# A decoder step on one core: projecting keys, queries, values in this order, and loading attention's first tiles during the last block

## The chip, the cores and the metric

One core of a Trainium2 chip runs the whole program. The metric is the device time of one execution in microseconds (us). Engine names: PE or TensorE (matmuls), PEld (its weight loads), DVE or VectorE, ACT or ScalarE, POOL or GpSimd, SP or SyncE (here it only issues transfers, "DMAs"). Each engine works through its own list of instructions in order and waits for the others by semaphores.

## The reference: what is computed

One inference step of a two-layer decoder for a prompt of 1024 tokens and eight sample tokens (1032 columns, width 1024). Layer 0 is a pooling mixer and a ConvFFN. Then one shared set of keys and values is projected, and layer 1 uses it with queries of its own in a dilated sliding-window attention with three groups of eight heads, followed by a second ConvFFN. What matters for the change:

```python
kv = einsum('btd,de->bte', rms_norm(x, g_kv), w_kv)       # keys and values, 3 groups x 8 heads x 64
k = rotary(rms_norm(kv[:, :, 0], k_gain), pos)            # keys: norm per head, then rotation
v = kv[:, :, 1]                                           # values: neither
q = einsum('btd,de->bte', rms_norm(x, g), w_q)
q = rotary(rms_norm(q, q_gain), pos) * (HEAD_DIM ** -0.5) # queries: like keys
```

The attention scores a block of 128 queries against its own block of keys and, in groups 0 and 1, the one before it, adds a mask, takes the exponential and weighs the values.

## The kernel before, in words

**Projection** (`pe_project`, `act_project`, `dve_project`, `pool_project`, `sp_project`; lines 1126 to 1372). Three groups `g`; in each three blocks `u`: keys (0), values (1), queries (2); in each nine tiles `t`: eight of 128 tokens and one with the eight sample rows. A full tile is 48 matmuls (two halves of 256 columns, eight slices of the width, three products of high and low parts; lines 1356 to 1358), the sample tile 32 narrower ones (lines 1352, 1353). The order of the last tiles is (7, half 0), (8, half 0), (7, half 1), (8, half 1). A tile's result lies in PSUM bank `t % 3`; a bank is free for tile `t + 3` when VectorE has written the row to `kn[t % 3]` (semaphore `pj_v`).

A key or query tile then goes a long way: ScalarE squares (L1240), VectorE sums per head (L1289), ScalarE takes a square root (L1243), VectorE refines it (L459 to L465, L1294) and scales into `kn` (L1297), GpSimd multiplies by the gain and rotates (L1321 to L1329), and SyncE stores the tile in device memory, in `kvs` or `qs` (L1157). A value tile needs one VectorE operation (L1283) and the store. A sample tile has ahead of that a ScalarE copy (L1224) and a VectorE sum (L1266). In each block ScalarE and VectorE also split four pieces of weights for the next block, at tiles 3, 5 and 7 (`pj_piece`, L1204 and L1206); SyncE loads them behind the stores of tiles 2, 5 and 8 (L1142). In the last group the last block splits and loads none. On TensorE group 0 is written out and groups 1 and 2 are a loop; on SyncE, ScalarE and VectorE groups 0 and 1 are the loop and the last group is written out.

**Attention** (`sp_attention`, `pe_attention`, `dve_attention`, `act_attention`, `pool_attention`). 24 steps `s` of one tile of queries and one of keys and values, 48 half steps `i` of four heads. TensorE transposes queries (`turn_q`) and keys (`turn_k`) into bank 7 (L1521), VectorE copies them to `qT` and `kT` (L1645), TensorE puts the mask (L1544) and the scores (L1552) into banks 0, 1 or 2, 3; VectorE takes the maxima (L1653), ScalarE the exponentials (L1760), TensorE transposes the probabilities (L1563) and multiplies by the values (L1579). Beside this GpSimd and VectorE multiply and sum the sample rows (L1782, L1681), from copies that SyncE loads.

SyncE's list behind the last projection store: it waits for TensorE's last projection matmul, for all weight pieces, and for all stores to have landed (L1433). Then it issues `load_q(0)` (L1439), `load_kv(0)` (L1445), `load_q(1)`, the masks (L1461), seven small loads of sample rows (L1463 to L1465), and in the loop over steps `load_q(s + 1)`, `load_kv(s)`, the store of step `s - 3` (L1510) and the sample rows' loads (L1452, L1455). From the third on, `load_q(s)` waits until the transposes of the queries two steps back are done; from the fifth on, `load_kv(s)` waits for outputs. VectorE begins the attention with four conversions, of the unit matrix and of the masks to bf16 (L1633 to L1639), for which it waits until the masks have landed; only then does it copy the first transposed queries. Masks, unit matrix and the tiles lie in SBUF over `xh` and `xl`, the projection's input, so they can't be filled before its last matmul.

Of the kernel before, what the change touches and what calls it, by code (L numbers as in the profile page):

```python
# [17 lines left out]
P = 128  # L18
# [6 lines left out]
KC = D // P  # L25
# [10 lines left out]
GROUPS = 3  # L36
# [21 lines left out]
def build(nc, a, o):  # L58

    with ExitStack() as ctx:  # L60
# [50 lines left out]
        osb = sb("osb", [P, 3, OW], F32, r1)  # L111
        maskf = sb("maskf", [P, 3, P], F32, r1)
        mask = sb("mask", [P, 3, QW], BF16, r1)
        identb = sb("identb", [P, P], BF16, r1)
        qn = sb("qn", [NS, GROUPS, QW], F32, r1)
# [51 lines left out]
        r2.close()  # L167
        wph, wpl = (wp0h, wp1h, wp2h), (wp0l, wp1l, wp2l)

        r2 = ExitStack()  # L170
# [955 lines left out]
        def pj_src(u, half, part, g, later):  # L1126
            cols = slice(half * HW, (half + 1) * HW)
            if u == 2:
                w = a["w_q"][0].rearrange("(k p) (g n) -> g p k n", p=P, g=GROUPS)
            else:  # L1130
                w = a["w_kv"].rearrange("(k p) (c g n) -> c g p k n", p=P, c=2, g=GROUPS)[u]
            return w[later:][bass.ds(g, 1), :, 4 * part:4 * part + 4, cols].rearrange("o p k n -> p (o k) n")

        def sp_project(sp):
# [9 lines left out]
            def body(g, last):  # L1144
                for u in range(3):
                    for t in range(9):
                        G = 27 * g + 9 * u + t
                        M = MT[t]
                        if u == 0 and t == 5:
                            sp.wait_ge(pj_l, 12 * g + 6)  # L1150
                        if u == 1:
                            sp.wait_ge(pj_v, G + (K0 + 1))
                        else:
                            sp.wait_ge(pj_r, 5 * (18 * g + (9 if u else 0) + t + 1))
                        rows = slice(t * P, t * P + M)
                        dst = qs[bass.ds(g, 1), rows, :] if u == 2 else kvs[bass.ds(g, 1), rows, u, :]
                        sp.dma_start(dst.rearrange("o p n -> (o p) n"), kn[0:M, t % 3, :]).then_inc(rows_out[t % 3], 16)  # L1157
                        for m in {2: [4 * u + 7], 5: [4 * u + 8], 8: [4 * u + 9, 4 * u + 10]}.get(t, []):
                            if m < 12 or not last:
                                load(m, g, free=(m == 8))  # L1160
# [24 lines left out]
        def pj_piece(e, g, m, act):  # L1185


            u, H, part = m % 12 // 4, m // 2, m % 2
            gain = G_ATTN if u == 2 else G_KV
            if act:  # L1190
# [25 lines left out]
        def act_project(act):  # L1216
# [9 lines left out]
            def body(g, last):  # L1226
                for u in range(3):
                    for t in range(9):
                        for m in pieces_at(u, t, last):
                            pj_piece(act, g, m, True)  # L1230
                        M, G = MT[t], 27 * g + 9 * u + t
                        if u != 1:
                            Q = 18 * g + (9 if u else 0) + t
                            act.wait_ge(pj_pe, G + 1)
                            act.wait_ge(pj_v, K0)
                            act.wait_ge(pj_s, 7 * Q + 1)
                            if t == 8:
                                sample_low(g, u)
                                act.wait_ge(pj_k, 6 * g + 2 * u + 2)
                            nc.scalar.activation(sq[0:M, 0, 0:QW], srow if t == 8 else ps[0:M, t % 3, :], ACT.Square,  # L1240
                                                 scale=rtok[0:M, t:t + 1]).then_inc(pj_sq, 1)
                            act.wait_ge(pj_s, 7 * Q + 3)
                            nc.scalar.activation(hs[0:M, 2, :], hs[0:M, 1, :], ACT.Sqrt).then_inc(pj_rt, 1)  # L1243
                        elif t == 8:
                            act.wait_ge(pj_pe, G + 1)
                            sample_low(g, u)
# [5 lines left out]
        def dve_project(v):  # L1252
# [16 lines left out]
            def body(g, last):  # L1269
                for u in range(3):  # L1270
                    for t in range(9):
                        for m in pieces_at(u, t, last):
                            pj_piece(v, g, m, False)
                        M, G = MT[t], 27 * g + 9 * u + t
                        b = t % 3
# [4 lines left out]
                        row = srow if t == 8 else ps[0:M, b, :]  # L1280
                        if u == 1:
                            v.wait_ge(pj_pe, G + 1)
# [20 lines left out]
            body(GROUPS - 1, True)  # L1303

        def pool_project(q):
            for i in range(3):
                q.wait_ge(rows_out[i], 16)
            half = HEADS * 8
            with q.Fori(0, GROUPS) as g:
                for u in (0, 2):  # L1310
                    for t in range(9):
# [101 lines left out]
        def wides(i):  # L1413
# [11 lines left out]
                    for r in range(T - WIN[g], N, P)]  # L1425

        def sp_attention(sp):

            sp.wait_ge(pj_pe, 27 * GROUPS)
            sp.wait_ge(pj_h, 12 * GROUPS)  # L1430
            sp.wait_ge(pj_l, 12 * GROUPS)
            for i in range(3):
                sp.wait_ge(rows_out[i], ROWS)  # L1433

# [22 lines left out]

            load_q(0)
            load_kv(0)
            load_q(1)  # L1460
            sp.dma_start(maskf[:, :, :], a["masks"]).then_inc(in_mask, 16)  # L1461
            for g in range(GROUPS):
# [3 lines left out]
            for s in range(NSTEP + 3):  # L1466
                if 1 <= s < NSTEP:
                    if s + 1 < NSTEP:
                        load_q(s + 1)
                    load_kv(s)  # L1470
                if s >= 3:
# [46 lines left out]
        def pe_attention(pe):  # L1518
# [5 lines left out]
            def turn_q(s):  # L1524
                pe.wait_ge(at_q[s % 2], moved(s, 2))
                wait(pe, at_tc, 2 * s)
                turn(qt[:, s % 2, :], s)

            def turn_k(s):
                pe.wait_ge(at_kv[s % 4], moved(s, 4))  # L1530
                pe.wait_ge(at_tc, 2 * s + 1)
                turn(kvt[:, s % 4, 0:QW], s)

            def scores(i):
# [5 lines left out]
                if i == 0:  # L1540
                    pe.wait_ge(at_mk, 4)
                m = 0 if wide(i) else (2 if STEPS[s][0] == 2 else 1)
                for c in range(2):
# [23 lines left out]
            def outputs(i):  # L1567
# [5 lines left out]
                for j in range(4):  # L1573
                    h = 4 * (i % 2) + j
                    tiles = [(s - 1) % 4, s % 4] if wide(i) else [s % 4]
                    for w, slot in enumerate(tiles):
                        n = j * len(tiles) + w
                        v = kvt[:, slot, QW + h // 2 * P:QW + (h // 2 + 1) * P]
                        mm = pe.matmul(ps[:, 6, j * P:(j + 1) * P], probT[:, i % 2, n * P:(n + 1) * P], v,  # L1579
# [51 lines left out]
        def dve_attention(v):  # L1631
            v.wait_ge(in_mask, 16)
            nc.vector.tensor_copy(identb[:, :], ident[:, :]).then_inc(at_mk, 1)  # L1633
            for m in range(3):
                if m == 0:
                    ins = nc.vector.tensor_copy(mask[:, 0, :].rearrange("p (w n) -> p w n", w=2),
                                                maskf[:, 0:2, :].rearrange("p c n -> p (c n)").unsqueeze(1).to_broadcast([P, 2, 2 * P]))
                else:
                    ins = nc.vector.tensor_copy(mask[:, m, 0:2 * P].rearrange("p (w n) -> p w n", w=2),  # L1639
                                                maskf[:, m, :].unsqueeze(1).to_broadcast([P, 2, P]))  # L1640
                ins.then_inc(at_mk, 1)

            def turned(s, k):
# [480 lines left out]
```

## Time and profile before

| | |
|---|---|
| time, median of 3 | 2437.13 us (2436.57 to 2438.08) |
| profiled execution | 2431.53 us, its span 2429.7 us |
| mean granted TensorE clock | 0.981 |
| TensorE busy | 2328.6 us, 96% of the span |
| VectorE, ScalarE, GpSimd busy | 1287.9, 758.5, 261.8 us |
| transfers | 273.34 MB, mean 112 GB/s |
| chain of work that ended last | PE 70%, issue 13%, POOL 6%, DVE 5%, DMA 3% |

Times of rows are in microseconds from the start of the span, durations of groups in nanoseconds where they say so. The busy time of a stretch tells which engine could bound it; the timeline tells when an instruction started, how long it took, and in brackets how long its engine had been idle before it and what ended that. "L1297" is a line of the kernel printed above; numbers such as "x2" count the instructions that are merged in a row, and the duration is then that of all of them.

### The profile page before, as it was taken

What the parts mean: (1) busy time and instruction counts of PE and PEld (TensorE: products, weight loads), DVE (VectorE), ACT (ScalarE), POOL (GpSimd) and SP (SyncE); (2) the same over time, 40 slices, a digit from 0 to 9 for tenths busy, and PEclk for the clock granted to TensorE, in tenths of its full rate; (3) what the DMA queues carried; (4) which work ended last, traced back from release to release, by engine and by line L of the source; (5) the groups of instructions that cost most, each with busy time, mean ns of one, the idle gap of its engine ahead of it and who ended that gap; (6) DMA issues with size and microseconds to landing.
All of it is one profiled execution on the core that took longest, in us unless ns stands there. A gap on an engine that the chain in (4) does not pass through costs nothing.

```text
span 2429.7 us, 41646 instructions
## 1 busy us (share of the span) xinstructions
PE 2328.6 (96%) x16141; PEld 2270.4 (93%) x16141; DVE 1287.9 (53%) x2088; ACT 758.5 (31%) x1345; POOL 261.8 (11%) x346
## 2 busy tenths in 40 slices
PE   7999999999999999999996989788999999999999
PEld 7899999999999899999996876587999999999999
DVE  5754554555455563645534775545545545554445
ACT  5422222223344431313212543232222222243333
POOL 1200000000011041523413220120000000000000
PEclk8999999999999999999998999899999999999999
DMA  5112212214654612222223787411222222245555
GB/s 172 35 52 78 78 52 78 78 53 144 199 169 153 210 54 97 84 97 71 79 71 112 240 254 205 162 33 44 59 71 78 61 69 78 59 148 190 192 169 175
DMA packets 198861, 273.34 MB, mean 112 GB/s; under 512 B 12424, under 2 KB 143800, under 8 KB 198483
## 3 DMA queue, kind: packets, MB, share of 16 engines
q1 hardware_dynamic: 193954, 267.09, 35.0%
q10 hardware_dynamic: 4792, 4.68, 0.6%
q8 instruction: 78, 1.28, 0.2%
q14 instruction: 37, 0.30, 0.0%
HBM read 218.19 MB, written 61.26 MB: 115 GB/s over the span
## 4 chain that ended last, share of the span: by engine, by line
PE 70%; issue 13%; POOL 6%; DVE 5%; DMA 3%; ACT 1%; SPq 1%; POOLq 0%; DVEq 0%; ACTq 0%
PE ps L337 43%; PE ps L814 18%; POOL kn L1321 3%; PE ps L1579 2%; PE ps L1552 1%; POOL sq L1323 1%; DMA kvt<-kvs 1%; POOL kn L1329 1%; PE ps L1563 1%; PE ps L1521 1%; PE ps L1591 1%; PE ps L646 1%; POOL sq L1324 1%; POOL sq L1326 1%; DVE rb L945 1%
## 5 line engine op out<-in xcount | busy, mean ns | idle before, releaser
L337 PE MATMUL ps<-xh,whl 128*128 128x344 f32 x4320 | 805.8, 321 | 16.2 <-DVE whl L777 11.9
L337 PEld LDWEIGHTS ps<-xh,whl 128*128 128x128 f32 x4320 | 703.2, 188 | 18.5 <-DVE whl L777 12.7
L337 PE MATMUL ps<-xl,whl 128*128 128x344 f32 x2160 | 459.3, 321 | 0.0
L814 PE MATMUL ps<-gdh,whl 128*128 128x384 f32 (+1 forms) x1568 | 377.7, 322 | 6.6 <-ACT ctm L898 3.0
L337 PEld LDWEIGHTS ps<-xl,whl 128*128 128x128 f32 x2160 | 366.6, 189 | 0.0
L814 PEld LDWEIGHTS ps<-gdh,whl 128*128 128x128 f32 x1568 | 273.6, 188 | 8.7 <-DVE gdl L983 3.8
L772 ACT ACTIVATE whl<-stage 128x1024 fp32r<-128x1024 f32 x88 | 93.1, 1060 | 515.0 <-DMA stage<-in_w_up 280.4
L814 PE MATMUL ps<-gdl,whl 128*128 128x384 f32 (+1 forms) x784 | 250.9, 320 | 0.0
L907 DVE TENSOR_TENSOR ub<-ps,rb 128x1032 f32<-128x1032 f32 x44 | 54.2, 1232 | 236.8 <-PE ps L337 236.8
L777 DVE TENSOR_TENSOR whl<-stage,whl 128x1024 fp32r<-128x1024 f32 x88 | 107.3, 1221 | 122.8 <-ACT whl L772 122.8
L814 PEld LDWEIGHTS ps<-gdl,whl 128*128 128x128 f32 x784 | 147.4, 188 | 0.0
L980 DVE TENSOR_TENSOR whl<-stage,whl 128x1024 fp32r<-128x1024 f32 x66 | 80.8, 1224 | 117.6 <-ACT whl L989 117.4
L814 PE MATMUL ps<-gdh,wx 128*128 128x384 f32 (+1 forms) x544 | 134.5, 316 | 0.0
L1760 ACT ACTIVATE prob<-ps,osb 128x128 f32<-128x128 f32 (+1 forms) x192 | 77.2, 414 | 140.1 <-DVE osb L1653 140.1
L1356 PE MATMUL ps<-wp0h,xh 128*128 128x256 f32 x384 | 110.1, 287 | 8.2 <-DVE x L999 6.0
L989 ACT ACTIVATE whl<-stage 128x1024 fp32r<-128x1024 f32 x66 | 70.0, 1060 | 136.4 <-PE ps L814 113.5
L922 DVE SCALAR_TENSOR_TENSOR cb<-ub,cwT,cb 128x1024 f32<-128x1024 f32 x88 | 112.4, 1277 | 0.0
L922 DVE SCALAR_TENSOR_TENSOR ca<-ua,cwT,ca 128x1024 f32<-128x1024 f32 x88 | 112.3, 1276 | 0.0
L1358 PE MATMUL ps<-wp0h,xl 128*128 128x256 f32 x384 | 110.1, 287 | 0.0
L1357 PE MATMUL ps<-wp0l,xh 128*128 128x256 f32 x384 | 109.4, 285 | 0.0
L907 DVE TENSOR_TENSOR ua<-ps,rb 128x1032 f32<-128x1032 f32 x44 | 54.2, 1233 | 101.9 <-PE ps L337 101.8
L1358 PE MATMUL ps<-wp1h,xl 128*128 128x256 f32 x384 | 108.2, 282 | 0.0
(258 smaller groups left out, 3970.3 us busy)
## 6 DMA issues: line engine op xcount, KB each, us to landing
stage<-in_w_down SPq DMA_DIRECT2D x100, 512.0 KB, 3.6
stage<-in_w_up SPq DMA_DIRECT2D x88, 512.0 KB, 5.3
gs<-cb SPq DMA_DIRECT2D x44, 516.0 KB, 3.1
graw<-gs SPq DMA_DIRECT2D x88, 192.0 KB, 3.6
rb<-in_w_down SPq DMA_DIRECT2D x32, 512.0 KB, 3.5
stage<-in_w_kv SPq DMA_DIRECT2D x24, 512.0 KB, 4.1
kvs<-kn SPq DMA_DIRECT2D x48, 256.0 KB, 2.0
kvt<-kvs SPq DMA_DIRECT2D x16, 512.0 KB, 4.6
```

Source lines behind the costliest of these rows:

```text
L337: mm = pe.matmul(ps[:, bank0 + c, 0:NW], w, m[:, c * NW:(c + 1) * NW], start=(i == 0), stop=(i == len(parts) - 1))
L772: nc.scalar.activation(wh[:, half, :], stage[:, half, :], ACT.Copy).then_inc(f_hi, 1)
L777: nc.vector.tensor_tensor(wl[:, half, :], stage[:, half, :], wh[:, half, :].bitcast(F32), ALU.subtract).then_inc(f_lo, 1)
L814: mm = pe.matmul(ps[:, d, 0:n], wt_, m, start=(f == 0 and i == 0), stop=(f == NF - 1 and i == 2))
L907: nc.vector.tensor_tensor(cols3(u[:, 2:2 + N]), bank3(half), cols3(rb[:, :]), ALU.mult).then_inc(S.B if half else S.A, 1)
L922: nc.vector.scalar_tensor_tensor(out=c[:, 0:T], in0=u[:, t:t + T], scalar=w, in1=c[:, 0:T], op0=ALU.mult, op1=ALU.add).then_inc(S.conv, 1)
L980: nc.vector.tensor_tensor(wdl[slot], draw[slot], wdh[slot].bitcast(F32), ALU.subtract).then_inc(f_dl, 1)
L1321: nc.gpsimd.tensor_tensor(row, row, per_head(hg[0:M, 1 if u else 0, :], HD), ALU.mult).then_inc(pj_r, 1)
L1356: pe.matmul(out, xh[:, k, tok], W[:, k, :], start=(k == 0), stop=False)
L1357: pe.matmul(out, xh[:, k, tok], Wt[:, k, :], start=False, stop=False)
L1358: mm = pe.matmul(out, xl[:, k, tok], W[:, k, :], start=False, stop=(k == KC - 1))
L1760: ins = nc.scalar.activation(prob[:, i % 2, j * n:(j + 1) * n], src[:, j % 2, j // 2, :], ACT.Exp, bias=osb[:, s % 3, QW + h:QW + h + 1], ...
```

## The change

The order of the blocks becomes keys, queries, values: `u` is 1 for queries and 2 for values in all five engines' projection functions. The masks, the unit matrix in bf16, the first queries (`qt0`) and the first keys and values (`kvt0`, over `rb`) get places that are free during the last block, and their loads stand in SyncE's list behind the store of the last block's tile 3, the four conversions in VectorE's list ahead of its tile 6. SyncE's attention list then starts with `load_q(1)` and `load_kv(1)`, for which it waits only for TensorE's last projection matmul, and waits for weight pieces and stores after these. TensorE's first two half steps wait for the last projection tiles to have left the banks. The diff, without the lines that only rename:

```diff
-        maskf = sb("maskf", [P, 3, P], F32, r1)
-        mask = sb("mask", [P, 3, QW], BF16, r1)
-        identb = sb("identb", [P, P], BF16, r1)
...
+        r2 = ExitStack()
+        sb("over_wp1", [P, 2 * KC, HW], F32, r2)
+        mask = sb("mask", [P, 3, QW], BF16, r2)
+        identb = sb("identb", [P, P], BF16, r2)
+        maskf = sb("maskf", [P, 3, P], F32, r2)
+        qt0 = sb("qt0", [P, QW], F32, r2)
+        r2.close()
+        kvt0 = rb[:, 0:2 * QW]
...
-            if u == 2:
+            if u == 1:
                 w = a["w_q"][0].rearrange("(k p) (g n) -> g p k n", p=P, g=GROUPS)
             else:
-                w = a["w_kv"].rearrange("(k p) (c g n) -> c g p k n", p=P, c=2, g=GROUPS)[u]
+                w = a["w_kv"].rearrange("(k p) (c g n) -> c g p k n", p=P, c=2, g=GROUPS)[u // 2]
...
                         sp.dma_start(dst.rearrange("o p n -> (o p) n"), kn[0:M, t % 3, :]).then_inc(rows_out[t % 3], 16)
+                        if last and u == 2 and t == 3:
+                            sp_first_tiles(sp)
...
-                        if u != 1:
+                        if u != 2:
                             Q = 18 * g + (9 if u else 0) + t
                             act.wait_ge(pj_pe, G + 1)
...
+                        if last and u == 2 and t == 6:
+                            dve_masks(v)
                         M, G = MT[t], 27 * g + 9 * u + t
...
+        def dve_masks(v):
+            v.wait_ge(in_mask, 16)
+            nc.vector.tensor_copy(identb[:, :], ident[:, :]).then_inc(at_mk, 1)
+            for m in range(3):
...
-                for u in (0, 2):
+                for u in (0, 1):
...
+        def q_tile(s):
+            return qt[:, s % 2, :] if s else qt0
+
+        def kv_tile(s):
+            return kvt[:, s % 4, :] if s else kvt0
+
+        def sp_first_tiles(sp):
+
+            for i in range(3):
+                sp.wait_ge(rows_out[i], 16 + 16 * 9)
+            sp.dma_start(maskf[:, :, :], a["masks"]).then_inc(in_mask, 16)
+            sp.dma_start(qt0[:, :], qs[0, 0:P, :]).then_inc(at_q[0], 16)
+            sp.dma_start(kvt0, kvs[0, 0:P].rearrange("t c n -> t (c n)")).then_inc(at_kv[0], 16)
+
         def sp_attention(sp):
 
             sp.wait_ge(pj_pe, 27 * GROUPS)
-            sp.wait_ge(pj_h, 12 * GROUPS)
-            sp.wait_ge(pj_l, 12 * GROUPS)
-            for i in range(3):
-                sp.wait_ge(rows_out[i], ROWS)
...
-            load_q(0)
-            load_kv(0)
             load_q(1)
-            sp.dma_start(maskf[:, :, :], a["masks"]).then_inc(in_mask, 16)
+            load_kv(1)
+            sp.wait_ge(pj_h, 12 * GROUPS)
+            sp.wait_ge(pj_l, 12 * GROUPS)
+            for i in range(3):
+                sp.wait_ge(rows_out[i], ROWS)
...
-                    load_kv(s)
+                    if s > 1:
+                        load_kv(s)
...
                 if i == 0:
                     pe.wait_ge(at_mk, 4)
+                if i < 2:
+                    pe.wait_ge(pj_v, 27 * GROUPS + K0 - 1 + i)
...
         def dve_attention(v):
-            v.wait_ge(in_mask, 16)
-            nc.vector.tensor_copy(identb[:, :], ident[:, :]).then_inc(at_mk, 1)
-            for m in range(3):
```

The waits of `sp_first_tiles` are for the stores of group 0, two groups back. The line `pj_v, 27 * GROUPS + K0 - 1 + i` stands for value tile 7 at the first half step and for the sample rows' values at the second.

## Rows read from the trace of the kernel before

**Rows 1.** Busy us (instructions) of PE, PEld, DVE, ACT, POOL; clock, DMA share, GB/s.

```profile
900.00:1000.00 100.00, 100.00 (x848) 99.83 (x847) 46.85 (x120) 23.23 (x54) 26.15 (x45) 1.00 0.26 88
1200.00:1299.20 99.20, 99.17 (x839) 98.75 (x837) 38.38 (x105) 16.08 (x38) 24.87 (x45) 1.00 0.18 60
1301.70:1325.20 23.50, 7.33 (x36) 5.23 (x37) 7.38 (x18) 3.84 (x12) 5.64 (x11) 0.50 0.40 118
```

**Rows 2.** Timeline of TensorE over the seam: start, us, engine, line, operation, tiles.

```profile
1298.90 0.28 PE L1353 MATMUL ps<-wp2l,xs 128*40 128x256 f32 x1
1313.54 1.12 PE L1521 MATMUL ps<-ident,qt 128*128 128x128 f32 x4 [14.36 <-DMA qt<-qs]
1318.21 1.08 PE L1521 MATMUL ps<-ident,kvt 128*128 128x128 f32 x4 [3.56 <-DVE qT L1645]
1320.08 0.61 PE L1544 MATMUL ps<-mask,identb 128*128 128x256 bf16 x2 [0.78 <-DVE kT L1645]
1321.77 1.11 PE L1521 MATMUL ps<-ident,qt 128*128 128x128 f32 x4
1324.40 1.10 PE L1521 MATMUL ps<-ident,kvt 128*128 128x128 f32 x4
1327.92 0.65 PE L1521 MATMUL ps<-ident,qt 128*128 128x128 f32 x4
```

**Rows 3.** Timeline of the other engines and of SyncE's issues over the seam.

```profile
1300.43 0.69 DVE L1297 TENSOR_TENSOR kn<-ps,hs 128x512 f32<-128x512 f32 x1
1310.81 0.35 SPq L1439 DMA_DIRECT2D qt<-qs  x1
1316.50 0.23 DVE L1633 CAST identb<-ident 128x128 bf16<-128x128 f32 x1 [10.17 <-DMA maskf<-in_masks]
1317.38 0.68 DVE L1645 COPY qT<-ps 128x512 f32<-128x512 f32 x1
```

**Rows 4.** The chain that ended last, over the seam: start, us, what.

```profile
1309.27 1.46 DMA qs<-kn
1312.15 4.33 DMA maskf<-in_masks
```

**Rows 5.** Timeline around the jump in TensorE's loop, and group 1's sample queries.

```profile
1149.82 0.38 PE L1356 MATMUL ps<-wp0h,xh 128*128 128x256 f32 x1 [2.18 <-issue]
1155.32 0.68 DVE L1297 TENSOR_TENSOR kn<-sq,hs 8x512 f32<-8x512 f32 x1
```

**Rows 6.** Timeline of a value block; L1240's first and last start; weight pieces.

```profile
919.45 1.67 DVE L1206 SCALAR_TENSOR_TENSOR wp1l<-stage,gT,wp1h 128x256 fp32r<-128x256 f32 x4
1240.70 0.75 DVE L1283 TENSOR_SCALAR kn<-ps,rtok 128x512 f32<-128x512 f32 x1 [4.94 <-PE ps L1358]
1251.14 0.59 ACT L1224 ACTIVATE sq<-ps 8x512 f32<-8x512 f32 x1 [2.46 <-DVE kn L1283]
1252.54 0.47 DVE L1283 TENSOR_SCALAR kn<-sq,rtok 8x512 f32<-8x512 f32 x1
L1240 ACT ACTIVATE sq<-ps,rtok x48: 667/688/690, 859.4 to 1297.4; 128x512 f32<-128x512 f32 x48
```

**Rows 7.** Landing of query tiles (L1439) and of key/value tiles (L1445).

```profile
DMA to landing us min/median/max: 2.7/5.1/9.2
...
DMA to landing us min/median/max: 3.6/4.9/9.9
```

**Rows 8.** Two gaps of TensorE in the attention, and the clock behind the first.

```profile
1406.04 0.66 PE L1521 MATMUL ps<-ident,kvt 128*128 128x128 f32 x4 [2.23 <-DMA kvt<-kvs]
1407.40:1410.65 3.25, 3.25 (x20) 2.78 (x18) 1.80 (x5) 0.95 (x3) 1.27 (x1) 0.50 0.34 122
1453.26 0.60 PE L1544 MATMUL ps<-mask,identb 128*128 128x512 bf16 x2 [2.77 <-DVE kT L1645]
```

**Rows 9.** Waits in the attention: who, for whom, us in all, times, longest.

```profile
SPq L1510 <- DVE osb L1664: 65.3, 14, 9.6
PE ps L1521 <- DMA kvt<-kvs: 9.4, 4, 5.6
```

More of the change, by code:

```diff
@@ L1150, in body @@
                             sp.wait_ge(pj_l, 12 * g + 6)
-                        if u == 1:
+                        if u == 2:
                             sp.wait_ge(pj_v, G + (K0 + 1))
@@ L1155, in body @@
                         rows = slice(t * P, t * P + M)
-                        dst = qs[bass.ds(g, 1), rows, :] if u == 2 else kvs[bass.ds(g, 1), rows, u, :]
+                        dst = qs[bass.ds(g, 1), rows, :] if u == 1 else kvs[bass.ds(g, 1), rows, u // 2, :]
                         sp.dma_start(dst.rearrange("o p n -> (o p) n"), kn[0:M, t % 3, :]).then_inc(rows_out[t % 3], 16)
+                        if last and u == 2 and t == 3:
+                            sp_first_tiles(sp)
                         for m in {2: [4 * u + 7], 5: [4 * u + 8], 8: [4 * u + 9, 4 * u + 10]}.get(t, []):
@@ L1188, in pj_piece @@
             u, H, part = m % 12 // 4, m // 2, m % 2
-            gain = G_ATTN if u == 2 else G_KV
+            gain = G_ATTN if u == 1 else G_KV
             if act:
@@ L1280, in body @@
                         row = srow if t == 8 else ps[0:M, b, :]
-                        if u == 1:
+                        if u == 2:
                             v.wait_ge(pj_pe, G + 1)
@@ L1303, in dve_project @@
             body(GROUPS - 1, True)
+        def dve_masks(v):
+            v.wait_ge(in_mask, 16)
+            nc.vector.tensor_copy(identb[:, :], ident[:, :]).then_inc(at_mk, 1)
+            for m in range(3):
+                if m == 0:
+                    ins = nc.vector.tensor_copy(mask[:, 0, :].rearrange("p (w n) -> p w n", w=2),
+                                                maskf[:, 0:2, :].rearrange("p c n -> p (c n)").unsqueeze(1).to_broadcast([P, 2, 2 * P]))
+                else:
+                    ins = nc.vector.tensor_copy(mask[:, m, 0:2 * P].rearrange("p (w n) -> p w n", w=2),
+                                                maskf[:, m, :].unsqueeze(1).to_broadcast([P, 2, P]))
+                ins.then_inc(at_mk, 1)
         def pool_project(q):
@@ L1526, in turn_q @@
                 wait(pe, at_tc, 2 * s)
-                turn(qt[:, s % 2, :], s)
+                turn(q_tile(s), s)
             def turn_k(s):
@@ L1531, in turn_k @@
                 pe.wait_ge(at_tc, 2 * s + 1)
-                turn(kvt[:, s % 4, 0:QW], s)
+                turn(kv_tile(s)[:, 0:QW], s)
             def scores(i):
@@ L1574, in outputs @@
                     h = 4 * (i % 2) + j
-                    tiles = [(s - 1) % 4, s % 4] if wide(i) else [s % 4]
-                    for w, slot in enumerate(tiles):
+                    tiles = [s - 1, s] if wide(i) else [s]
+                    for w, tile in enumerate(tiles):
                         n = j * len(tiles) + w
-                        v = kvt[:, slot, QW + h // 2 * P:QW + (h // 2 + 1) * P]
+                        v = kv_tile(tile)[:, QW + h // 2 * P:QW + (h // 2 + 1) * P]
                         mm = pe.matmul(ps[:, 6, j * P:(j + 1) * P], probT[:, i % 2, n * P:(n + 1) * P], v,
@@ L1631, in dve_attention @@
         def dve_attention(v):
-            v.wait_ge(in_mask, 16)
-            nc.vector.tensor_copy(identb[:, :], ident[:, :]).then_inc(at_mk, 1)
-            for m in range(3):
[L1635 to L1641, printed above, removed]
             def turned(s, k):
```

## The prediction

> **What bounds the kernel now.** I began with the busy time by stretch [rows 1]. Up to 1299.20 us TensorE is busy all the time (99.17 of 99.20 us) at the full clock; behind it, from 1301.70 to 1325.20, it is busy for 7.33 of 23.50 us. The projection is bound by TensorE, the seam behind it is not. Next I read TensorE's own timeline over the seam [rows 2]: the last projection matmul ends at 1298.90 + 0.28 = 1299.18, the first query transposes start at 1313.54, the key transposes at 1318.21, and the first scores (with their mask) at 1320.08. So 1320.08 - 1299.18 = 20.90 us pass between the projection's end and the first scores.
>
> What fills them is in the chain of waits and in the timelines of the other engines [rows 3, 4]. Queries are projected last, so the normalization and rotation of their last two tiles lie at the end: tile 7's queries leave VectorE at 1300.43 + 0.69 = 1301.12, the eight sample rows go the same way one after another through ScalarE, VectorE and GpSimd, and their store starts at 1309.27 and lands at 1309.27 + 1.46 = 1310.73. Only then does SyncE issue the first loads: queries at 1310.81, then keys/values, and masks at 1312.15. The first tile is there at 1313.5, the masks at 1312.15 + 4.33 = 1316.48, and VectorE, which must convert the masks before it copies anything for TensorE, copies the first queries at 1317.38.
>
> **The change part by part.**
>
> *Order keys, queries, values.* The same matmuls, the same operations for each tile; TensorE's projection keeps its length if it meets no new wait. New is that a query block follows a key block inside a loop body: two blocks with the long chain side by side. The trace already has this neighbourhood between groups (queries, then the next group's keys). There the sample rows' keys or queries are finished at 1155.32 + 0.68 = 1156.00 [rows 5]; the block had ended at 1147.64 (1149.82 less the idle 2.18), that is 8.4 us earlier. TensorE wants that bank (three banks, nine tiles) at the next block's tile 2, two tiles or 11.4 us behind the block's end (48 matmuls of a tile at 848 in 100 us [rows 1] are 5.66 us). So 3.0 us are to spare, without counting the 2.18 us of the loop's jump. Cost 0; the cover is TensorE's own work on two tiles.
>
> *What is left behind the last matmul.* Now the last block is values: tile 7 needs one VectorE operation, which starts about when the corresponding ScalarE one did, 1297.4 [rows 6], and takes 0.75. The sample rows take ScalarE copy, VectorE sum, VectorE scale: from 1251.14 to 1252.54 + 0.47 = 1253.01, 1.87 us [rows 6]. TensorE's results are visible some 0.2 us after 1299.18, so VectorE is free at 1299.4 + 1.87 = 1301.3. GpSimd and the square root drop out of the path.
>
> *First tiles, masks.* The three loads are issued after value tile 3, some four and a half tiles (25 us) ahead of the end, against a slowest landing of 9.9 us for such tiles and 4.33 for the masks [rows 4, 7]. In the projection's last part SyncE only stores. Their three issues (0.35 us for one, [rows 3]) stand ahead of the store of value tile 4, which comes a tile later (5.66 us): nobody waits. The four conversions (1317.38 - 1316.50 = 0.88 us, [rows 3]) move ahead of value tile 6, where VectorE is idle for 4.94 us in each tile [rows 6]. All this costs 0.
>
> *The new seam, summed.* TensorE transposes the first queries right at 1299.2 (0.65 us at the full clock, 1.12 at the lower). VectorE copies them at 1301.3 (0.68) to 1302.0; TensorE takes 0.15 to start (1318.21 - 1317.38 - 0.68, [rows 2, 3]): keys' transposes at 1302.15. From there to the first scores it is as before, 1320.08 - 1318.21 = 1.87: 1304.0. The value tiles 7 and 8, whose banks the first scores now wait for, are done by 1298.2 and 1301.3. Gain 1320.08 - 1304.0 = **16.1 us**.
>
> *The clock.* It was at the lower level, 0.50 (1.2 of 2.4 GHz), from 1301.70 to 1325.20 [rows 1], after 2.5 us of idleness and until 5.1 us into steady work. The new seam holds two idle pieces of some 2.3 and 1 us. The trace has both outcomes for such a gap: after 2.23 us idle the clock was 0.50 for 3.25 us, after 2.77 us it stayed at 1.00 [rows 8]. At 1.00 the keys' transposes and copy would be 0.45 shorter (0.65 for 1.12, [rows 2]). The first two half steps take TensorE 1324.40 - 1321.77 = 2.63 us each now, and half of that at 1.00; but VectorE's reduce, copy, reduce, copy of some 0.68 each [rows 3] behind about 1.1 us of scores then ends last, at 3.9 us (an estimate from these rows), against 5.3: 1.4 us, or up to 2.0 with the later transposes. So the clock adds 0 (as low as before) to 0.45 + 2.0 = 2.5 us. I take 0.5: the first 5 us behind 1301.7 look much as before, with short work between waits. The Trainium skill (TensorE: Matmul & The Clock Gate, The HAM clock gate) states that the throttled level is the default and that sustained activity releases it; by that alone the start would run low, and the sum would stay at 16.1. The gap of 2.77 us that left the clock high shows that a gap of this size does not settle it.
>
> *Who is next.* SyncE stores the sample values at 1301.35 (0.3), then tile 1's queries at about 1301.8 and its keys/values at 1302.2, landing at best 2.7 and 3.6 us later [rows 7]: 1304.5 and 1305.8. They are wanted at 1304.0 + (1321.77 - 1320.08) = 1305.7 and 1304.0 + (1324.40 - 1320.08) = 1308.3 [rows 2]. Then SyncE waits for the sample store (1301.4 + 1.5 = 1302.9, over by then) and issues the seven small loads, at 0.35 each [rows 3] 2.4 us, and tile 2's queries at about 1305.0, landing at 1307.7 to 1310.1 (median 5.1); wanted at 1304.0 + (1327.92 - 1320.08) = 1311.9. Everything later hangs on TensorE's progress: SyncE waited 65.3 us for the outputs of steps whose rows it stores [rows 9], so the loads move along with them, as does the sample rows' work. The stage's later waits for transfers (9.4 us, [rows 9]) move and are not filled. The layer behind it starts from the attention's end.
>
> *Exit from TensorE's loop.* Before, whatever it cost lay under 14.36 us of waiting. Bounds: the jump back cost 2.18 us [rows 5], running into the loop, between 998 and 1000, nothing (TensorE is busy for all of the 100 us to 1000, [rows 1]); leaving is nearer to the latter, as no jump is taken, so 0. If 2.18: transposes end at 1302.5 instead of 1299.9, VectorE copies 1.2 us later than summed. The Trainium skill (Runtime: NRT & Kernel Launch, Instruction fetch mechanics) says that a taken branch can force a fetch of the target, and that running on is prefetched; by that rule it is 0.
>
> *Sum.* 16.1 + 0.5 = **16.6 us**. The profiled execution took 2431.53 (span 2429.7), the timed ones 2437.13; I carry the difference in us over: 2437.13 - 16.6 = **2420.5**, and 2413.1 for the new span. A change within 0.2% (4.9 us) is about what a measurement can't tell from none.
>
> **The rivals.**
>
> *Clock high throughout the new start:* 16.1 + 2.5 = 18.6 us, 2418.5. For it: the 2.77 us gap. Against: the low clock at the old seam began 2.5 us after the end of steady work. Chance 0.10.
>
> *SyncE late with tile 2 or tile 1.* All small loads now stand between the value tile and tile 2's queries, close to their use. If those take the slowest landing, 9.2 us [rows 7], they arrive at 1314.2 instead of 1311.9, 2.3 us late; tile 1's keys/values at 9.9 would be 3.8 late. Some 4 us gone: gain 12.6, 2424.5. For it: landing times grow where tiles share the queues; against: these come before the sample loads start. Chance 0.09.
>
> *Given back in the transfer-bound part.* Later in the stage TensorE waits four times for keys and values, 5.6 us at most [rows 9]. If transfers there don't keep pace with the earlier start and one more such wait appears, the gain is 16.6 - 5.6 = 11, 2426. Against: all issues follow TensorE's events. Chance 0.05.
>
> *No change, since something else holds the start,* for instance a wait at the first scores for a late projection tile in place of the old ones. It would have to last over 11.7 us; the value chain's length of 1.87 speaks against. 2436. Chance 0.02.
>
> *Slower.* The long chain in two neighbouring blocks falls behind TensorE. A tile's chain now runs from ScalarE's 1297.4 to 1300.43 + 0.69 = 1301.12, 3.7 us, plus weight pieces (four of 1.67 us in nine tiles, [rows 6]), 4.5 in all against 5.66 per tile. Above 5.66 a backlog grows; over 8 tiles in each of 3 groups it eats the 16.6 us from 5.66 + 16.6/24 = 6.35 us on. If GpSimd, ScalarE and VectorE, now active together for two blocks on end, slowed each other to 6.5 per tile: 24 x 0.84 = 20.2 lost, 3.6 us slower, 2440.7. Against: query blocks next to key blocks keep up today. Chance 0.02.
>
> **How the numbers follow.** The forecast has 0.72: 2420.5, its own range 2418.5 to 2423 (loop exit 1.2, landing times 1, clock 2). With the high clock (0.10) below and SyncE's lateness (0.09) above, 2417.5 to 2425.0 leaves out the giving back, no change, slower and some of each end, under 2 in 10. Faster by over 0.2%: 0.72 + 0.10 + 0.09 + 0.05 less a little of the last, 0.95; within 0.2%: 0.03; slower: 0.02.
>
> **What would show it.** Right: TensorE busy throughout the projection with its end unmoved near 1299; first query transposes within 0.3 us; first scores 4.8 us behind the end; no wait for the masks; the rest of the attention shifted as a block. Wrong: idle time of the projection's matmuls behind VectorE in the query block; TensorE waiting for tile 1 or tile 2; more than 9.4 us of waiting for keys/values later; the interval from first scores to the attention's end longer than before.

## The result, and the profile after

| | before | after |
|---|---|---|
| median | 2437.61 us (2436.57 to 2440.27, 4 runs) | 2416.97 us (2411.69 to 2420.93, 4 runs) |
| ratio | | 0.9917 (95%: 0.99 to 0.9933) |
| profiled execution, its span | 2431.53, 2429.7 us | 2411.69, 2409.9 us |
| mean granted clock | 0.981 | 0.985 |

The forecast was 2420.5 in 2417.5 to 2425.0. The change is faster, as forecast, but 20.6 us in place of 16.6, and 0.5 us below the range. Two later comparisons gave ratios of 0.9922 (0.9908 to 0.9937) and 0.993 (0.9913 to 0.9947), gains of 17.1 and 17.4 us by medians. So part of the 20.6 is scatter: over all comparisons single executions of the kernel before lie up to 15 us apart (2428.99 to 2443.86), those of the changed kernel up to 12 (2411.63 to 2423.23). The three comparisons together give some 18.4 us, 1.8 above the forecast. The rest of this text is about where the traces differ from the forecast's terms.

TensorE's timeline over the new seam, to be read against [rows 2] (columns as there; `rb` is now the first keys and values):

```profile
1297.91 0.28 PE L1374 MATMUL ps<-wp2l,xs 128*40 128x256 f32 x1
1298.03 0.60 PE L1555 MATMUL ps<-ident,qt 128*128 128x128 f32 x4
1300.85 0.63 PE L1555 MATMUL ps<-ident,rb 128*128 128x128 f32 x4 [2.22 <-DVE qT L1670]
1302.27 0.39 PE L1580 MATMUL ps<-mask,identb 128*128 128x256 bf16 x2 [0.79 <-DVE kT L1670]
1303.73 1.11 PE L1555 MATMUL ps<-ident,qt 128*128 128x128 f32 x4
1306.24 0.66 PE L1555 MATMUL ps<-ident,kvt 128*128 128x128 f32 x4
1307.93 0.38 PE L1580 MATMUL ps<-mask,identb 128*128 128x512 bf16 x1 [0.59 <-DVE kT L1670]
```

The 14.36 us of waiting are gone, the query transposes follow the last matmul at once, and the first scores start at 1302.27, 4.08 us behind 1297.91 + 0.28 = 1298.19. The other engines and SyncE, to be read against [rows 3, 4]:

```profile
1298.23 0.59 ACT L1231 ACTIVATE sq<-ps 8x512 f32<-8x512 f32 x1 [42.44 <-PE ps L1374]
1298.92 0.68 DVE L1273 TENSOR_TENSOR sq<-sq,ps 8x512 f32<-8x512 f32 x1 [1.71 <-ACT sq L1231]
1299.63 0.47 DVE L1292 TENSOR_SCALAR kn<-sq,rtok 8x512 f32<-8x512 f32 x1
1300.03 0.67 DVE L1670 COPY qT<-ps 128x512 f32<-128x512 f32 x1
1300.47 0.35 SPq L1470 DMA_DIRECT2D qt<-qs  x1
1300.86 0.43 SPq L1476 DMA_DIRECT2D kvt<-kvs  x1
```

The chain is the one of the forecast: ScalarE copy, VectorE sum, VectorE scale, then the copy of the first queries; no masks, no GpSimd. The busy time by stretch, against [rows 1], with the clock in the third column from the right:

```profile
1200.00:1298.20 98.20, 98.20 (x833) 98.06 (x832) 45.52 (x119) 16.83 (x39) 32.42 (x56) 1.00 0.20 71
1298.20:1302.20 4.00, 1.06 (x8) 0.61 (x6) 2.43 (x4) 1.87 (x2) 0.00 (x0) 1.00 0.29 89
1302.20:1306.30 4.10, 4.04 (x25) 3.01 (x26) 1.39 (x3) 1.51 (x8) 0.00 (x0) 0.58 0.87 243
```

In this trace the clock stays high through the seam's waits and falls to 1.2 GHz behind them, in the first two half steps. And the waits of the later attention, against [rows 9]:

```profile
SPq L1544 <- DVE osb L1689: 63.0, 14, 9.1
PE ps L1555 <- DMA kvt<-kvs: 8.2, 5, 4.4
```

8.2 us of waiting for keys and values where 9.4 had been: nothing was given back there.

To see where the whole difference lies, I cut each trace at the same instructions: first and last matmul of the projection, first scores, first scores of the third half step, last scores, first output projection matmul, end. Lengths in us, for three traces of either kernel (two later ones of each from the experiments):

| stretch | before, 3 traces | after, 3 traces | mean difference |
|---|---|---|---|
| ahead of the projection | 846.8, 850.4, 850.2 | 847.8, 850.8, 852.0 | +1.1 |
| projection | 452.4, 452.5, 452.4 | 450.4, 448.8, 450.3 | -2.6 |
| seam | 20.90, 21.67, 21.45 | 4.08, 4.07, 4.07 | -17.3 |
| two half steps | 6.21, 5.59, 5.78 | 5.67, 6.45, 5.39 | 0.0 |
| rest of the attention | 211.2, 214.0, 210.8 | 209.6, 213.0, 214.5 | +0.3 |
| merge of the groups | 60.3, 62.3, 60.0 | 60.6, 61.9, 61.6 | +0.5 |
| output projection, second ConvFFN | 832.0, 831.8, 831.9 | 831.8, 832.5, 831.8 | +0.2 |

Only two rows differ by more than they scatter: seam and projection. The sum is -17.8 us, in agreement with the later comparisons.

### The profile page after: what moved, and what is told of

It is laid out like the page before. It is cut to its first block, busy times and chain, and to the rows that moved or that the text cites. A ratio compares the mean times of both kernels' runs of the same rounds, so it can differ in the third digit from the quotient of the medians.

```text
span 2409.9 us, 41632 instructions
## 1 busy us (share of the span) xinstructions
PE 2326.3 (97%) x16130; PEld 2269.7 (94%) x16141; DVE 1294.0 (54%) x2088; ACT 759.3 (32%) x1345; POOL 263.3 (11%) x346
## 4 chain that ended last, share of the span: by engine, by line
PE 89%; DVE 5%; DMA 3%; ACT 1%; SPq 1%; issue 1%; POOL 0%; DVEq 0%; ACTq 0%; POOLq 0%
PE ps L342 44%; PE ps L819 18%; PE ps L1379 6%; PE ps L1377 6%; PE ps L1378 6%; PE ps L1615 2%; PE ps L1588 1%; DMA kvt<-kvs 1%; PE ps L1627 1%; PE ps L1599 1%; PE ps L1555 1%; PE ps L651 1%; PE ps L1374 1%; PE ps L1373 1%; DVE rb L950 1%
```

## The experiments

Theory A: the seam alone makes the gain, the rest is a clock term taken too small and scatter. Theory B: the new order itself shortens the projection. Later, J: what the order gives in the projection lies in one place, the jump of TensorE's loop; against it K: the jump's part is chance, and the order works elsewhere.

**The two kernels again.** Unchanged.

> The kernel before once more, against itself. Theory A (the changed seam alone makes the gain; the 4 us above the forecast are a clock term taken too small and scatter between executions): ratio 1.000, and its timed runs scatter by some 4 us; in the trace the seam from the last projection matmul to the first scores is again 20.9 us within 0.3, while the stretches outside of it differ from the first trace by up to 2 us in sum. Theory B (the new order itself shortens the projection by 2 us): the projection's length, first to last matmul, is 452.4 us again within 0.3.

> The changed kernel once more, five rounds. A: ratio 0.9925 to 0.993 (a gain of 17 to 18.5 us: seam 16.8, clock in the first half steps 0 to 2), not the 20.6 of the first medians; the seam 4.1 us; the projection's length 451 to 453. B: the projection's length 450.4 again within 0.3, the gain 19.5 to 21 us, ratio 0.9915 to 0.992.

Measured: the kernel before against itself 1.0007 (0.9994 to 1.002), its ten runs from 2428.99 to 2443.86 us; the kernel after 0.9922. The projections were 452.5 and 448.8 us. The seam of before was 21.67, 0.8 longer, which A had not allowed; that of after 4.07. The scatter is larger than I had thought, and B had the better of it on the projection, though its number, 450.4 again, was missed too, and the ratio is A's. The projection must be looked at block by block.

**Order alone.** The diff of `pj_src`, `sp_project`, `pj_piece`, `act_project`, `dve_project` and `pool_project`, nothing of the loads:

```diff
-                        if u != 1:
+                        if u != 2:
                             Q = 18 * g + (9 if u else 0) + t
...
-                for u in (0, 2):
+                for u in (0, 1):
```

> Only the order keys, queries, values; first loads and masks as before. Both theories take the seam as the sum of a chain: the sample values leave VectorE 2.1 us behind the last matmul, their store lands 1.8 us later, and from there 9.35 us pass to the first scores as before (1320.08 - 1310.73): 13.2 us in place of 20.9. A: gain 7.7 us, ratio 0.9968. B: 9.7 us, ratio 0.9960, the projection 2 us shorter.

Measured: ratio 0.9961 (0.9946 to 0.9975), seam 13.88 us for 13.2 expected, projection 448.8. TensorE over its seam:

```profile
1307.56 1.11 PE L1521 MATMUL ps<-ident,qt 128*128 128x128 f32 x4 [5.95 <-DMA qt<-qs]
1313.62 1.09 PE L1521 MATMUL ps<-ident,kvt 128*128 128x128 f32 x4 [4.95 <-DVE qT L1645]
1315.49 0.61 PE L1544 MATMUL ps<-mask,identb 128*128 128x256 bf16 x2 [0.79 <-DVE kT L1645]
```

With the long chain gone, the first load (5.95 us) and the masks (4.95 us, in which VectorE waits for them) remain. The ratio says 9.5 us, near B's 9.7, but its interval holds A's 7.7 too, and the medians differ by 7.6. It is the length of the projection, 3.6 us less than before, that speaks for B, and 1.3 of these 3.6 will turn out to lie in the first block.

**Early loads alone.** The order keys, values, queries, all else as in the changed kernel: the diff above with its signs exchanged.

> Only the early tiles and masks, the order keys, values, queries as before. The long chain of the sample queries holds VectorE until 7.1 us behind the last matmul; then copy 0.7, transposes and copy 2.0: first scores 9.8 us behind the end in place of 20.9, a gain of 11 us there. Tile 1, loaded behind the sample queries' store (issued at 10.1 us), lands at 13 (queries) and 14.5 (keys/values) where 11.5 and 14 are wanted: 1.5 to 2 us back. A: gain 9 to 9.5 us, ratio 0.9962. B: the same, since it holds nothing of the order's 2 us. Order alone and loads alone together give less than both, if A is right: 7.7 + 9.3 = 17 against 16.8 would be a coincidence of two chains that overlap only in part.

```profile
1298.48 0.60 PE L1555 MATMUL ps<-ident,qt 128*128 128x128 f32 x4
1306.55 1.09 PE L1555 MATMUL ps<-ident,rb 128*128 128x128 f32 x4 [7.47 <-DVE qT L1670]
1308.42 0.61 PE L1580 MATMUL ps<-mask,identb 128*128 128x256 bf16 x2 [0.79 <-DVE kT L1670]
1311.86 1.11 PE L1555 MATMUL ps<-ident,qt 128*128 128x128 f32 x4 [1.68 <-DMA qt<-qs]
```

Ratio 0.9964 (0.995 to 0.9977), seam 9.78 us for 9.8 expected, and the late tile 1 appears, 1.68 us. Each half of the change alone leaves the other's chain on the path. By the seams, against the mean of before (21.34): order 7.5, loads 11.6 less 1.7, both 17.3.

**Masks late.** The changed kernel with the masks loaded behind tile 1 and converted at the start of VectorE's attention:

```diff
@@ sp_attention
             load_kv(1)
+            sp.dma_start(maskf[:, :, :], a["masks"]).then_inc(in_mask, 16)
@@ dve_attention
+            dve_masks(v)
```

> The changed kernel, but masks loaded behind the projection (behind tile 1's loads) and converted at the start of VectorE's attention, as before; order and first tiles stay early. The masks are issued 3.7 us behind the last matmul, land 4.3 later, conversion 0.9, queries' copy 0.7, keys' transposes and copy 2.0: first scores 11.6 us behind the end in place of 4.1, so the masks' place is worth 7.5 us; the tile 1 loads are then never late. Time against before: 16.8 + 2 - 7.5 = 11 us, ratio 0.9953. Rival: if the masks land sooner, as only two other loads are under way, in 3 us, 10.3 us and 12.5 in all.

Ratio 0.9947 (0.9928 to 0.9965), seam 12.24 us for 11.6 expected, as the masks landed 5.5 us after their issue and not 4.3: their early place is worth 8.2 us of the seam. VectorE says who was late:

```profile
DVE identb L1314 <- DMA maskf<-in_masks: 6.7, 1, 6.7
```

**TensorE's loop written out,** in the changed kernel and in the one before:

```diff
-            with pe.Fori(1, GROUPS) as g:
+            for g in range(1, GROUPS):
                 body(g, False)
```

> The changed kernel with TensorE's projection loop written out, so that TensorE jumps nowhere. So far nine blocks of the projection take 49.19 us each in every trace, except the one with the jump: 53.15 and 53.30 before, 51.17 and 50.88 after. Theory J (what the order gave in the projection, 2.0 to 3.7 us, lies wholly in that jump: its idle time and a stretch of low clock behind it): all blocks take 49.19, the projection from first to last matmul 447.0 to 447.3, so 1.7 to 2 us less than in the changed kernel; gain against before 19 to 21 us. Theory K (the order frees VectorE or TensorE elsewhere, and the jump is chance): the block keeps some of its 1.7 to 2.0 us.

> The kernel before, old order, with the same loop written out. J: the same 49.19 in all blocks and 447.0 to 447.3 in all, as in the changed kernel written out, so 4 to 5 us less than before (452.4): ratio 0.998. The seam stays 20.9 to 21.6 us. K: the block in question stays longer by the 2 us that the order gave.

The distances between the last matmuls of neighbouring blocks are 49.17 to 49.20 us in every trace of every kernel, save at the jump (the last traces of either kernel, from further down, are included):

| | block with the jump | idle at it | low clock behind it |
|---|---|---|---|
| before, 3 traces | 53.16, 53.30, 53.18 | 2.18, 2.34, 2.20 | 3 of 3 |
| early loads alone (old order) | 51.65 | 2.20 | no |
| after, 3 traces | 51.17, 50.88, 51.08 | 1.72, 1.44, 1.64 | none |
| order alone, small matmuls in the seam (new order) | 50.93, 51.17 | 1.48, 1.72 | no |
| masks late (new order) | 52.88 | 1.92 | yes |
| written out, old and new order | 49.18, 49.18 | 0 | no |

Written out, the projection's blocks behind the first are alike in both orders, as J says; the totals are 448.4 and 447.4 us for the 447.0 to 447.3 expected. The rest of the difference between traces is the first block: 54.86 to 54.90 us in ten traces, 53.59 to 53.86 in four (the second trace of the changed kernel, order alone, the changed kernel written out, and the loads below without small matmuls), which lack one stretch of 3.4 us at 1.2 GHz. All five traces of the old order have the long one, five of nine of the new; whether the order has a part in that is not shown. Of the 2.6 us by which the projection is shorter on the mean, 2.2 are at the jump and 0.4 in that first block of one trace.

Ratios to before: 0.9972 (0.9956 to 0.9988) for the old order, 0.9892 (0.9871 to 0.9912) for the changed kernel, which is by this ratio 26 us of gain where 19 to 21 were expected. The same 12 us around the jump, before (first line), after (second) and the kernel before written out (third), columns as in [rows 1]:

```profile
1148.00:1160.00 12.00, 10.19 (x73) 10.19 (x74) 7.06 (x24) 2.62 (x6) 5.49 (x10) 0.86 0.08 25
```

```profile
1148.00:1160.00 12.00, 10.28 (x87) 10.01 (x86) 5.22 (x14) 1.49 (x3) 0.00 (x0) 1.00 0.36 113
```

```profile
1148.00:1160.00 12.00, 12.00 (x104) 11.97 (x103) 9.23 (x26) 4.72 (x11) 3.71 (x7) 1.00 0.12 45
```

Before, TensorE idles and then runs 3.4 us at 1.2 GHz (0.86 on the mean); after, it idles for a little less and keeps 2.4 GHz. The stretch costs 1.5 us: with the same idle time of 2.20 us the block took 53.18 us with it and 51.65 without.

**Keeping TensorE at work in the seam.** The changed kernel with small matmuls into a bank that is not yet in use:

```diff
+            def fill(n):
+                for _ in range(n):
+                    pe.matmul(ps[:, 4, 0:P], identb[:, :], mask[:, 1, 0:P], start=True, stop=True)
             turn_q(0)
+            pe.wait_ge(at_mk, 4)
+            fill(34)
             turn_k(0)
+            fill(12)
```

> The changed kernel with 34 and 12 small matmuls into an unused bank in the two waits of the new seam, which changes no wait and keeps TensorE at work. It prices the clock at the seam. If the low clock behind the seam (3.4 to 6.8 us at 0.50, from 1302.2 on) comes from these waits: it disappears, first scores 4.0 us behind the end, from there to the third half step 4.2 to 4.6 us in place of 5.6 to 6.5, so 1.2 to 2 us less. If the clock falls all the same: as after. The time itself scatters by 4 us and can hardly show it; the trace decides.

```profile
1302.58 0.39 PE L1580 MATMUL ps<-mask,identb 128*128 128x256 bf16 x2
1303.55 0.66 PE L1555 MATMUL ps<-ident,qt 128*128 128x128 f32 x4
1304.35 0.72 PE L1588 MATMUL ps<-kT,qT 64*128 64x128 f32 x8
1307.39 0.66 PE L1555 MATMUL ps<-ident,kvt 128*128 128x128 f32 x4 [2.32 <-DMA kvt<-kvs]
1308.83 1.03 PE L1580 MATMUL ps<-mask,identb 128*128 128x512 bf16 x2 [0.35 <-DVE kT L1676]
```

The low clock was gone from the two half steps (0.66 for the transposes that took 1.11), yet they took 6.25 us, no less than without: TensorE reached tile 1's keys and values before these had landed. And behind that wait of 2.32 us the clock was at 1.2 GHz after all, for 3.4 us from 1308.83 on (1.03 us for a mask that takes 0.60 at the full clock): the fourth half step began 15.3 us behind the last projection matmul, against 12.9 to 13.8 in the changed kernel's three traces. I had foreseen only the clock, not the transfer. Ratio 0.9919 (0.9899 to 0.9939), as the changed kernel.

**Both, and the loop.** Tile 1's loads issued right behind the last matmul, ahead of the sample values' store; the loop written out; without and with the small matmuls:

```diff
+                            if last and t == 8:
+                                sp_second_tiles(sp)
                             sp.wait_ge(pj_v, G + (K0 + 1))
...
+        def sp_second_tiles(sp):
+            sp.wait_ge(pj_pe, 27 * GROUPS)
+            sp.dma_start(qt[:, 1, :], qs[0, P:2 * P, :]).then_inc(at_q[1], 16)
+            sp.dma_start(kvt[:, 1, :], kvs[0, P:2 * P].rearrange("t c n -> t (c n)")).then_inc(at_kv[1], 16)
```

> The same without the small matmuls. Clock low for 3.4 us or more behind the seam as in the changed kernel; seam 4.1, from first scores to third half step 5.4 to 5.6, no wait for tile 1. The difference to the one with small matmuls is the clock alone: 1 to 1.4 us.

> The changed kernel with three additions: TensorE's projection loop written out; tile 1's queries and keys/values issued right behind the last matmul, ahead of the sample values' store; and the small matmuls in the two waits of the seam. Theory: with the clock kept high TensorE was stopped by tile 1's keys and values (2.32 us of waiting, asked for 3.3 us behind the last matmul); asked for 2 us earlier they are there in time. Seam 4.1 us, from first scores to third half step 4.2 to 4.6 us in place of 5.4 to 6.5, projection 447.3: 4 us less than the changed kernel, ratio to before 0.989 to 0.9905. Rival: loads take the longer landing beside each other and TensorE waits again, 5.5 us as before; then the filler is worth nothing and the gain is the 2 us of the loop.

With the small matmuls, the third half step began 3.94 us behind the first scores (1300.32 to 1304.26):

```profile
1300.32 0.39 PE L1585 MATMUL ps<-mask,identb 128*128 128x256 bf16 x2
1302.84 0.63 PE L1560 MATMUL ps<-ident,kvt 128*128 128x128 f32 x4
1304.26 0.60 PE L1585 MATMUL ps<-mask,identb 128*128 128x512 bf16 x2
```

Without them 5.37 us: the clock's price there is 1.4 us, as the prediction had estimated it (3.9 against 5.3), and it is only to be had once the transfer is earlier. In the time it does not show: 2410.15 us (2407.77 to 2413.23), ratio 0.9896 (0.9879 to 0.9912) without, 2412.65 us (2407.91 to 2415.94), 0.9906 (0.989 to 0.9921) with, for 0.989 to 0.9905 expected (its first block was a long one, so its projection took 448.4 us and not 447.3). Against the changed kernel of the same comparison (2418.86 us) the first is 8.7 us less by medians. Of this the traces' projections account for 3.2 us (450.3 and 447.1; 1.9 of it the jump, the rest the first block). The other 5.5 us are not located. The remaining attention alone varies by 5 us among traces of one kernel, so scatter may be enough; but all three changed kernels with the loop written out have medians of 2410.2 to 2412.7, against 2417.0 to 2418.9 in the three comparisons of the changed kernel, so it may be more than scatter. Both are faster than the changed kernel by medians, and the loop written out is the part that the traces show.

**The changed kernel and the one before, a third time.**

> The changed kernel a third time, for the jump in TensorE's loop and for the ratio. Idle time at the jump so far 1.7, 1.4 us (and 1.5, 1.9, 1.7 in three relatives with the new order) against 2.2, 2.3, 2.2 in the old order. If the order shortens it: again under 2.0. Low clock right behind the jump, which costs 1.7 us, came in 2 of 3 traces of the old order and 1 of 5 of the new one: chance. Ratio 0.992, a gain of 19 us.

> The kernel before a third time, for the same. Idle time at the jump above 2.1 us if the order decides it; anything from 1.4 to 2.3 if it is chance. Seam 20.9 to 21.9 us.

```profile
1153.24 0.38 PE L1356 MATMUL ps<-wp0h,xh 128*128 128x256 f32 x1 [2.20 <-issue]
```

2.20 us in the old order, 1.64 in the new: in ten traces with the jump it was 2.2 to 2.3 in the four of the old order and 1.4 to 1.9 in the six of the new. This small part goes with the order. The low clock behind the jump came in 3 of 4 and in 1 of 6. The changed kernel's ratio was 0.993, 17.4 us for the 19 expected; the kernel before gave 1.0002 against itself, with a seam of 21.45 us.

The traces hold one more thing about the jump. In all ten a 16 KB transfer on the queue that brings instructions (q8) starts shortly ahead of TensorE's idle time, 0.3 to 0.4 us ahead in the old order and 1.1 in the new. It takes 0.96 to 1.43 us, and in the new order the idle time is its length plus 0.5 in all six traces (0.96 and 1.44 us in the shortest case, 1.43 and 1.92 in the longest), in the old order plus 1.2 to 1.4. So the new order's shorter idle time goes with an earlier start of this transfer, and its spread with the transfer's length.

## Why the prediction was off, step by step

- **Where the seam's time lies, and what removes it: right.** The old seam was filled by the sample queries' chain, the first load and the masks; all three left it. Half the change alone left the other half's chain, as the two single edits show.
- **The new seam, 4.8 us forecast, 4.1 measured.** ScalarE started 0.04 us behind the last matmul's end, not 0.2; VectorE's copy of the queries began at 1300.03, 1.84 us behind that end (2.1 in the sum), as ScalarE started earlier and neighbouring VectorE operations overlap a little; and keys' transposes to first scores took 1.42 us, not 1.87, since the clock had not fallen yet. That last 0.45 was in the text as a part of the clock's term.
- **The old seam, 20.9, was one sample.** Two more traces gave 21.7 and 21.5. The masks landed in 5.1 and 4.9 us there, 4.33 in [rows 4], which is the whole difference. The seam's gain was 17.3 us on the mean for 16.1 forecast. A wait that ends with a transfer should have had a range on both sides; mine was counted as exact.
- **"Cost 0" for the projection: wrong, the step that failed.** I asked only whether the order adds a wait, and bounded that term from above. No wait was added (two tiles are 11.3 us and not 11.4, which changes nothing), but the block with the jump of TensorE's loop became 2.2 us shorter on the mean of three traces: 0.6 us of idle time and a stretch at 1.2 GHz worth 1.5 us. The whole projection is 2.6 us shorter, with 0.4 from the first block of one trace. The expectations' 2.0 to 3.7 us at the jump and 1.7 us for the stretch were too much. The row for it was there, [rows 5], with 2.18 us; I used it only for the loop's exit, where it cost nothing, as taken, and did not look at the clock behind it.
- **The clock, +0.5: nothing.** Before, the clock was low from inside the seam's wait until 3.4 to 5.3 us behind the first scores (three traces); after, it is low for 3.4 to 6.8 us, from about the first scores on. The two half steps took 5.4 to 6.5 us, 5.8 on the mean, as before. The seam's 0.45 of that term came in. That the half steps would give another 1.4 to 2.0 with the clock high was wrong for this kernel: with it high, tile 1's keys and values were late by 2.32 us. I had their landing at 1305.8 at best against 1308.3 wanted, with the half steps at the low clock; the rival of SyncE's lateness and that of the high clock were one case, not two.
- **Who is next, what is carried on: right.** No wait for tile 1 or 2 in the changed kernel, no more waiting for keys and values later, the second layer as before within 0.2 us on the mean. Slower, no change and giving back did not happen.
- **The range.** It held the mechanism's terms, not the scatter. The kernel before alone ran from 2429 to 2444 us, though its first three runs lay within 1.5 us; a median of four can be 2 us off by that. The range's lower end lay only 1.0 us under the best case of one term (2418.5) and left little room for another term with the sign of a gain. As a gain the range was 12.1 to 19.6 us. The two later ones, 17.1 and 17.4, lie in it, so the first, 20.6, owes its place outside in part to scatter; by the traces the seam and the projection together would give 19.9, and the other stretches took 2.1 back, none of them by more than it scatters.

What stays open: why the transfer of instructions at the jump starts 0.7 us earlier, and the idle time is shorter, when a value block precedes it. TensorE's own instructions are the same in the kernel with the order alone and in the one before, and only what the other engines and the transfers do at that time differs. The low clock behind it goes with the longer idle time, but one trace (1.92 us) has it and one (2.20) hasn't, so its cause is argued, not shown.

## What to carry to other kernels

When two stages meet, put last in the first stage what needs the least work after its matmuls, and load the second stage's first operands and constants into places that are free before the end; do both, since each alone leaves the other's chain on the path. Bound every term of a moved piece on both sides, also those that seem untouched: cut two or three traces at the same instructions and see which stretches scatter. And before paying to keep the clock high, look whether a transfer ends the same wait.

## What the runs showed of the hardware

- A backward jump in TensorE's list cost 1.4 to 2.3 us of idleness in the middle of dense matmuls, and 1.5 us more where a stretch of 3.4 us at 1.2 GHz followed. Writing the loop out removed all of it. Running into the loop and leaving it cost nothing: the transposes began 0.12 us after the last matmul's start. The Trainium skill (Runtime: NRT & Kernel Launch, Instruction fetch mechanics) says that instructions are prefetched in sequence, and that a taken branch whose target is not in the pages at hand has to fetch it before execution goes on. The traces agree: idle time at the jump only, and together with a 16 KB transfer of instructions.
- A block of 416 matmuls took 49.17 to 49.20 us in every trace, save the first and the one with the jump, while whole executions of the same kernel scattered by 12 to 15 us. The scatter lies in the stretch ahead of the projection, the first block, the attention and the merge. Slower executions have the lower mean granted clock (0.981 at 2423.2 us, 0.986 at 2411.6, changed kernel), and a late start of the projection goes with more time at 1.2 GHz ahead of it (16 to 20 us for starts at 846.8 to 848.2, 24 to 27 us for starts at 850.2 to 852.8, fourteen traces). Which of the two is the cause is not shown.
- The low clock began 3.2 to 4.5 us behind the last projection matmul in the changed kernel's three traces, each time while TensorE was working, and 2.3 to 5.2 us behind it in the three of before, in the wait. It was absent from the first two half steps when small matmuls filled the waits, and came behind the next wait, of 2.32 us.
